# The experts' w1 and w3 laid out in pairs of rows: 4 KB DMA runs where there were 2 KB

## The chip, the cores and the metric

The kernel runs as one program on one core of a Trainium2 chip. The metric is the device time of an execution in microseconds (us), the median of three runs. One execution was taken by the hardware profiler; all rows in this document up to the prediction come from that execution. It reports the engines PE (TensorE matmuls), PEld (its weight loads), DVE (VectorE), ACT (ScalarE), POOL (GpSimd), SP (SyncE, which here only issues DMAs) and the core's 16 DMA engines.

## The reference

One step of a hybrid decoder for 2048 prompt tokens and 8 x 4 sample tokens, D = 1024, all float32: stick-breaking attention beside an RG-LRU, an output projection, and then the part that matters here, a mixture of 32 experts of which each token uses two:

```python
def expert_block(args):
    toks, e = args
    xb = x_pad[toks]
    hb = jax.nn.silu(xb @ w1[e]) * (xb @ w3[e])   # w1, w3: 1024 x 512
    return hb @ w2[e]                             # w2: 512 x 1024
...
out = out.reshape(n_rows, d) * row_gate[:, None].astype(x.dtype)
return jax.ops.segment_sum(out, row_tok, num_segments=n_tok + 1)[:n_tok]
```

Every expert's w1, w3 and w2 are 2 MB each (2048 KB), 6.29 million bytes (MB) in all, and are read from HBM once. A final residual add and RMSNorm end the step.

## The kernel before

The phases follow one another: modulation, input projection, attention, then `router_experts_phase`, then `final_phase`. The router writes each token's row twice into scratch tensors in HBM, `xs_d0` and `xs_d1` (half a row each), sorted by expert. `experts_of` then goes through the 32 experts in order and, for each, through as many blocks of 64 rows as that expert has (a loop with a register as its bound; it is one block for some experts and four for others).

A block n needs these steps, each on an engine of its own:

- POOL, `load(n)`: four DMAs of 64 KB bring the block's rows from `xs_d` into `x_in` (it lies in `rowsP`, two buffers), line L1935. Each of the four parts has a semaphore of its own, and `hold` makes POOL wait, before it issues a part, until the same part of the block before has landed. So only one DMA of each part is under way at a time.
- POOL, `store(n)`: two DMAs of 128 KB write a finished block to `ys_d`, L1949. Before it issues them POOL waits until both DMAs of the store before have landed. Loads and stores alternate in POOL's order.
- ACT, `landed(n + 1)`: when all four parts have landed, one copy of the rows into `o_rs` (L1987); DVE turns it into `xT` (in `o_sq`, L2051).
- PE, `hidden`: x times w1 and w3, L2016. The work is cut into strips: 64 calls for a block, which stand as 128 records. ACT and DVE form silu and the product (L1992, L2056 to L2060).
- PE, `out`: the hidden rows times w2, L2023, 64 records. ACT copies the result into `y` (L1997).

The weights come on SP's queue into three slots: `w13_0` to `w13_2` hold w1 and w3 together, `w2_0` to `w2_2` hold w2. In the trace's names `w13_0` and the `w2` slots stand as `w`, `w13_1` lies in `oT` and `w13_2` in `w_out`. SP issues, for expert e, the two DMAs of w1 and w3 (2048 KB each, L1913) once `hidden` of expert e - 3 has freed the slot, and then four DMAs of 512 KB for w2 (L1922) once expert e - 3 is finished. PE waits for an expert's w1 and w3 before its first block and for its w2 before `out`. Expert 0's weights are loaded ahead, during the router. After expert 31's weights SP loads `x1_d` rows for the final phase (L1926 to L1931) into slots that come free.

In w13 partition p holds eight rows of w1 and w3, rows 8p to 8p + 7, of 2 KB each; row c of w1 lies beside row c of w3. w2's rows are 4 KB.

Of the kernel before, what the change touches and what calls it, by code (L numbers as in the profile page):

```python
# [15 lines left out]
P = 128  # L16
D = 1024
KC = D // P
# [15 lines left out]
DE = D // 2  # L34
# [3 lines left out]
Q = P // STRIPS  # L38
# [272 lines left out]
def emptied(n, engine):  # L311

    return sum(e == engine for _, e in JOBS[:n + 1])
# [532 lines left out]
def attention_phase(nc, io, keep, sems):  # L846
# [15 lines left out]
    def place(n):  # L862

        return divmod(n - FIRST, WINDOW) if n >= FIRST else (-1, 0)

    EVENTS = []
    for n in range(TICKS):
        unit, p = place(n)
# [15 lines left out]

    with ExitStack() as stack:
        k = Kit(nc, stack)
        shared = keep["w13_0"][:, :, :, :].rearrange("p c a n -> p (c a n)")
        kT = [shared[:, SEQ * i:SEQ * i + SEQ] for i in range(2)]
        qT = [shared[:, SEQ * (2 + i):SEQ * (2 + i) + SEQ] for i in range(2)]
        vv = [k.sb(f"vv{i}", [P, NT, P]) for i in range(2)]  # L890
# [34 lines left out]
        ident, oT = keep["ident"], keep["oT"]  # L925
# [497 lines left out]
def router(nc, io, keep, sems, k):  # L1423
# [6 lines left out]
    w_out = keep["w_out"]  # L1430
# [8 lines left out]
    t1, xT = mid[:, 2 * D:3 * D], mid[:, 3 * D:].rearrange("p (c n) -> p c n", c=KC)  # L1439
# [32 lines left out]
    ident, oT = keep["ident"], keep["oT"]  # L1472
# [10 lines left out]
    def sync(sp):  # L1483
        sp.dma_start(nf_row[:, :], io["norm_ffn"].to_broadcast([P, D])).then_inc(s["small"], 16)

        def load_x(i):
            if i == 0:
                sp.dma_start(x_t[0][0:NS, :], io["x_sample"].rearrange("b t n -> (b t) n")).then_inc(s_x[0], 16)
            else:
                sp.dma_start(x_t[i % 2][:, :], x_src[i - 1]).then_inc(s_x[i % 2], 16)  # L1490

        def load_rg(i):
            sp.dma_start(featT[i % 2][:, FC:, :], rgT[i - 1]).then_inc(s_rg[i % 2], 16)

        load_rg(1)
        load_x(0)
        sp.dma_start(w_r[:, :, 0:NG], io["w_group"][0].rearrange("(c p) n -> p c n", p=P)).then_inc(s["wr"], 16)
        sp.dma_start(w_r[:, :, 8:RW], io["w_router"][0].rearrange("(c p) n -> p c n", p=P)).then_inc(s["wr"], 16)
        sp.dma_start(b_r[:, 0:NG], io["b_group"].to_broadcast([P, NG])).then_inc(s["small"], 16)
        sp.dma_start(b_r[:, 8:RW], io["b_router"].to_broadcast([P, NE])).then_inc(s["small"], 16)  # L1500
        load_x(1)
        load_rg(2)
        for at, name in enumerate(("w1", "w3")):
            sp.dma_start(keep["w13_0"][:, :, at, :], io[name][0, 0].rearrange("(p c) n -> p c n", p=P)).then_inc(sems["pre"], 16)
        for i in range(NTL):
            sp.wait_ge(s["x1"], i + 1)
            sp.dma_start(io["x1_d"][row0[i]:row0[i] + size[i], :], x1[i % 2][0:size[i], :]).then_inc(s_st[i % 2], 16)
            if i + 2 < NTL:
                load_x(i + 2)
            if i >= 1 and i + 2 < NTL:  # L1510
                sp.wait_ge(s["mm1"], i + 1)
                load_rg(i + 2)
        for b in range(2):
            sp.wait_ge(s_st[b], 16 * len(range(b, NTL, 2)))
# [337 lines left out]
def experts_of(nc, io, keep, sems, k, emptied, gates_scalar, gates_vector):  # L1852
# [7 lines left out]
    w13, w2 = [keep[f"w13_{i}"] for i in range(SLOTS)], [keep[f"w2_{i}"] for i in range(SLOTS)]  # L1860
    x_in = keep["rowsP"][:, 2, :].rearrange("p (a n) -> p a n", a=2)
    x_turn = keep["o_rs"][:, :, :].rearrange("p c n -> p (c n)")
    xT = keep["o_sq"][:, :, :].rearrange("p c n -> p (c n)").rearrange("p (c u b) -> p c u b", c=KC, u=UNITS)
# [3 lines left out]
    yb, h = keep["banks"][3], [keep["banks"][b] for b in (4, 6)]  # L1867
# [4 lines left out]
    s_w13 = [k.sem(f"p7_w13{i}") for i in range(SLOTS)]  # L1872
    s_w2 = [k.sem(f"p7_w2{i}") for i in range(SLOTS)]
    src = {n: io[n][0] for n in ("w1", "w3", "w2")}
# [17 lines left out]
    def sync(sp):  # L1892
        done = sp.alloc_register("blocks_done")
        sp.reg_mov(done, 0)
        emptied(sp, "low")
        for j in range(EC):
            sp.dma_start(w2[0][:, j, :], src["w2"][0].rearrange("(p j) n -> j p n", p=P)[j]).then_inc(s_w2[0], 16)
        sp.wait_ge(sems["placed"], 1)
        for landed in s_in:
            sp.wait_ge(landed, 32)  # L1900
        for e in range(NE):
            i = e % SLOTS
            if e == 1:
                emptied(sp, "oT")
            if e == 2:
                emptied(sp, "w_out")
            if e >= SLOTS:
                sp.reg_add(done, done, blocks_of(sp, e - SLOTS))
                freed = sp.snap(done, min_val=1, max_val=MAX_BLOCKS)
                hold(sp, s["h1"], freed, s["sp"])  # L1910
            if e > 0:
                for at, name in enumerate(("w1", "w3")):
                    sp.dma_start(w13[i][:, :, at, :], src[name][e].rearrange("(p c) n -> p c n", p=P)).then_inc(s_w13[i], 16)  # L1913
            if e == 1:
                emptied(sp, "mid")
            if e == 2:
                emptied(sp, "high")
            if e >= SLOTS:
                hold(sp, s["y"], freed, s["sp"])
            if e > 0:  # L1920
                for j in range(EC):
                    sp.dma_start(w2[i][:, j, :], src["w2"][e].rearrange("(p j) n -> j p n", p=P)[j]).then_inc(s_w2[i], 16)  # L1922
        x1_rows = io["x1_d"][0:SEQ, :].rearrange("(t p) n -> p t n", p=P)
        sp.reg_add(done, done, blocks_of(sp, NE - 3))
        hold(sp, s["y"], sp.snap(done, min_val=1, max_val=MAX_BLOCKS), s["sp"])
        sp.dma_start(keep["x1_a"], x1_rows[:, 0:8, :]).then_inc(sems["x1_a"], 16)  # L1926
        sp.dma_start(keep["x1_b"], x1_rows[:, 8:12, :]).then_inc(sems["x1_b"], 16)
        sp.reg_add(done, done, blocks_of(sp, NE - 2))
        hold(sp, s["y"], sp.snap(done, min_val=1, max_val=MAX_BLOCKS), s["sp"])
        sp.dma_start(keep["x1_c"], x1_rows[:, 12:16, :]).then_inc(sems["x1_c"], 16)  # L1930
        sp.dma_start(keep["x1_s"], io["x1_d"][SEQ:, :]).then_inc(sems["x1_s"], 16)  # L1931
# [79 lines left out]
    def tensor(pe):  # L2011
        def hidden(i, u):

            for c in range(KC):
                for q in range(STRIPS):
                    mm = pe.matmul(h[u][q * Q:q * Q + Q, 0:2 * P], xT[:, c, u, :], w13[i][:, c, :, q * P:q * P + P], start=(c == 0), stop=(c == KC - 1))  # L2016
            return mm

        def out(i, u):

            for j in range(EC):
                for q in range(STRIPS):
                    mm = pe.matmul(yb[q * Q:q * Q + Q, u * (XW // 2):(u + 1) * (XW // 2)], hT[:, u, j, :], w2[i][:, j, q * (XW // 2):(q + 1) * (XW // 2)],  # L2023
                                   start=(j == 0), stop=(j == EC - 1))
            return mm

        def body(n, e, b, extra):
            i = e % SLOTS
            for u in range(UNITS):
                pe.wait_ge(s["xT"], 2 * n + u + 2)  # L2030
                hidden(i, u).then_inc(s[f"h{u}"], 1)
            pe.wait_ge(s_w2[i], 16 * EC * (e // SLOTS + 1))
            for u in range(UNITS):
                pe.wait_ge(s["hT"], 2 * n + u + 1)
                mm = out(i, u)
            mm.then_inc(s["y"], 1)

        def before(e):
            i = e % SLOTS
            if e == 0:  # L2040
                pe.wait_ge(sems["pre"], 32)
            else:
                pe.wait_ge(s_w13[i], 32 * (e // SLOTS + (1 if i else 0)))

        pe.wait_ge(sems["placed"], 1)
        experts(pe, body, before)
# [177 lines left out]
def build_program(nc, io):  # L2224
    with ExitStack() as stack:
        k = Kit(nc, stack, clears=False)
        keep = {
            "ident": k.sb("ident", [P, P]), "ones": k.sb("ones", [P, P]), "eps": k.sb("eps", [P, 1]),
            "vecT": k.sb("vecT", [P, NVEC]), "biasP": k.sb("biasP", [P, H]), "nbiasP": k.sb("nbiasP", [P, H]),
        }  # L2230
# [4 lines left out]
        sems = {f"w_{part}": k.sem(f"w_{part}") for part in WCOL}  # L2235
# [25 lines left out]
        keep["rowsP"] = k.sb("rowsP", [P, 4, D])  # L2261
        rows_s = k.sb("rowsS", [P, 4, D])
        keep["rowsS"], keep["rows_mem"] = rows_s[0:NS, :, :], (keep["rowsP"], rows_s)
        keep["w13_0"] = k.sb("w13_0", [P, KC, 2, DE])
        keep["oT"], keep["w_out"] = k.sb("oT", [P, FC, SEQ]), k.sb("w_out", [P, 2, KC, 512])
        for name in ("w_out0", "w_out1", "rows", "x1_a", "x1_b", "x1_c", "x1_s"):
            sems[name] = k.sem(name)
        attention_phase(nc, io, keep, sems)
        for i in range(3):
            keep[f"w2_{i}"] = k.sb(f"w2_{i}", [P, EC, D])  # L2270
        keep["w13_1"] = keep["oT"][:, :, :].rearrange("p f n -> p (f n)").rearrange("p (c a n) -> p c a n", c=KC, a=2)
        keep["w13_2"] = keep["w_out"][:, :, :, :].rearrange("p h c n -> p (h c n)").rearrange("p (c a n) -> p c a n", c=KC, a=2)
        tiles = lambda t: t[:, :, :, :].rearrange("p c a n -> p c (a n)")
        keep["x1_a"], keep["x1_b"] = tiles(keep["w13_2"]), keep["w2_2"][:, :, :]
        keep["x1_c"], keep["x1_s"] = tiles(keep["w13_0"])[:, 0:4, :], tiles(keep["w13_0"])[0:NS, 4, :]
        keep["yy"] = tiles(keep["w13_1"])
# [35 lines left out]
```

## Time and profile before

| what | value |
|---|---|
| median of 3 runs | 2826.22 us (2825.38 to 2827.81) |
| the profiled execution, its own time | 2821.11 us |
| its span, first to last instruction | 2819.6 us |
| its mean granted PE clock | 0.969 |
| PE busy | 2586.6 us (92%) |
| first `hidden` of the experts to the end of the last `out` | 1842.40 to 2724.58 us |
| moved over the whole span | 577.06 MB, mean 205 GB/s |

The experts' stretch is some 31% of the span. PE busy is near its whole length in most of it, and the DMA engines are near full as well, so that an average over the span does not say which of the two sets the pace: that has to be read in pieces. A DMA share over 1.00 means that packets of different queues overlap on an engine.

### The profile page before, as it was taken

Reading aid. Unit: us, or ns where it says so; the run is one execution under the profiler, and the core shown is the slowest. Engines: PE = TensorE matmul, PEld = TensorE weight load, DVE = VectorE, ACT = ScalarE, POOL = GpSimd, SP = SyncE. Lnnn points to the kernel's source line nnn. Section 1 sums busy time; section 2 is a strip of 40 time slices with the busy share of each in tenths; the row PEclk is TensorE's granted clock in tenths of the full one; section 3 lists DMA queues with packets and bytes.
Section 4 is the critical chain, followed back from the end, with each engine's and each line's share of the span. In section 5 each row is a group of like instructions: output and inputs, shape, how many; then the busy total and the mean of one; then the engine's idle time right before and its main releaser. Section 6 shows DMA issues by size and latency. Waiting matters only on the chain. (4 is left out here: it accounts for less than half of the span.)

```text
span 2819.6 us, 64656 instructions
## 1 busy us (share of the span) xinstructions
PE 2586.6 (92%) x23589; PEld 1361.0 (48%) x23589; DVE 1379.9 (49%) x2816; ACT 1055.4 (37%) x1938; POOL 648.4 (23%) x918
## 2 busy tenths in 40 slices
PE   6999999996799899899998999789999998899978
PEld 3444444442455445454543555445555554555533
DVE  2151423333678788687886777522222222222228
ACT  2221314121677777687773222122222221122214
POOL 0202020101021211111111222343333333333333
PEclk9999999998899999999999999899999999999989
DMA  9011111126586766767675344399999789999947
GB/s 335 15 61 44 45 45 43 62 85 244 174 271 218 264 234 224 262 213 244 225 262 187 116 140 139 143 261 295 281 301 299 210 257 306 323 309 297 305 134 315
DMA packets 297027, 577.06 MB, mean 205 GB/s; under 512 B 80278, under 2 KB 96727, under 8 KB 292812
## 3 DMA queue, kind: packets, MB, share of 16 engines
q1 hardware_dynamic: 194472, 427.99, 47.4%
q0 software_dynamic: 102016, 146.26, 16.9%
q8 instruction: 116, 1.90, 0.3%
q14 instruction: 99, 0.81, 0.1%
q10 hardware_dynamic: 324, 0.10, 0.0%
HBM read 461.12 MB, written 112.29 MB: 203 GB/s over the span
## 5 line engine op out<-in xcount | busy, mean ns | idle before, releaser
L1253 DVE TENSOR_TENSOR_SCAN left<-leave,left 128x512 f32<-128x512 f32 (+3 forms) x320 | 358.4, 1120 | 134.9 <-ACT leave L1135 134.1
L442 PE MATMUL bank<-xnT,w_in 128*128 128x512 f32 x768 | 330.3, 592 | 0.0
L2056 DVE TENSOR_TENSOR sg<-sg,bank 128x128 f32<-128x128 f32 x160 | 46.0, 288 | 562.5 <-ACT sg L1992 561.3
L2023 PE MATMUL bank<-w,hT 128*32 128x256 f32 x5120 | 297.5, 380 | 1.5 <-issue 1.1
L1056 POOL DMA_DIRECT2D w_out<-in_cache_v x256 | 137.6, 538 | 660.9 <-issue 658.6
L1935 POOL DMA_DIRECT2D rowsP<-xs_d x328 | 218.0, 665 | 200.0 <-DMA rowsP<-xs_d 111.4
L2016 PE MATMUL bank<-w,o_sq 128*32 128x256 f32 x3840 | 218.0, 384 | 30.2 <-DVE o_sq L2051 23.2
L442 PEld LDWEIGHTS bank<-xnT,w_in 128*128 128x128 f32 x768 | 145.6, 190 | 181.8 <-issue 178.9
L1992 ACT ACTIVATE sg<-bank 128x128 f32<-128x128 f32 x160 | 44.4, 278 | 501.2 <-PE bank L2016 501.2
L1619 PE MATMUL bank<-w_out,w 128*128 128x512 f32 x512 | 227.7, 597 | 1.8 <-DVE w L1683 1.8
L442 PE MATMUL bank<-w_in,xnT 128*128 128x512 f32 x512 | 220.4, 592 | 0.0
L2023 PEld LDWEIGHTS bank<-w,hT 128*32 128x32 f32 x5120 | 160.1, 110 | 124.2 <-DVE hT L2060 25.7
L2016 PE MATMUL bank<-oT,o_sq 128*32 128x256 f32 x3712 | 205.8, 379 | 7.1 <-DVE o_sq L2051 7.1
L1304 PE MATMUL tb<-ident,take 128*128 128x128 f32 x1088 | 181.7, 284 | 29.5 <-DVE take L1159 25.7
L1135 ACT ACTIVATE leave<-zb,nbiasP 128x512 f32<-128x512 f32 (+3 forms) x320 | 204.6, 639 | 8.0 <-PE zb L1297 8.0
L1137 ACT ACTIVATE take<-zb,biasP 128x512 f32<-128x512 f32 (+3 forms) x320 | 207.3, 648 | 0.0
L1159 DVE TENSOR_TENSOR take<-take,left 128x512 f32<-128x512 f32 (+3 forms) x320 | 194.6, 608 | 15.5 <-DVE left L1253 0.4
L1949 POOL DMA_DIRECT2D ys_d<-y x164 | 115.6, 709 | 365.3 <-DMA ys_d<-y 180.8
L1291 PE MATMUL zb<-w 64*128 64x512 f32 (+3 forms) x640 | 164.1, 590 | 31.0 <-ACT take L1137 19.9
L1304 PEld LDWEIGHTS tb<-ident,take 128*128 128x128 f32 x1088 | 119.8, 142 | 146.7 <-issue 77.4
L1339 PE MATMUL tb<-ident,w_out 128*128 128x128 f32 x1024 | 159.9, 280 | 25.3 <-DMA w_out<-in_cache_k 15.7
L2016 PEld LDWEIGHTS bank<-w,o_sq 128*32 128x32 f32 x3840 | 125.2, 111 | 118.2 <-DVE o_sq L2051 26.3
(408 smaller groups left out, 3402.1 us busy)
## 6 DMA issues: line engine op xcount, KB each, us to landing
w_out<-in_cache_v POOLq DMA_DIRECT2D x256, 256.0 KB
w_out<-in_cache_k SPq DMA_DIRECT2D x256, 256.0 KB
w<-in_w SPq DMA_DIRECT2D x128, 512.0 KB, 17.4
w<-in_w SPq DMA_DIRECT2D x22, 2048.0 KB, 23.1
oT<-in_w SPq DMA_DIRECT2D x22, 2048.0 KB, 24.2
w_out<-in_w SPq DMA_DIRECT2D x20, 2048.0 KB, 25.7
ys_d<-zeros SPq DMA_DIRECT2D x32, 816.0 KB
ys_d<-y POOLq DMA_DIRECT2D x166, 128.0 KB, 7.8
```

Of the source, the lines that this page charges most:

```text
L442: mm = pe.matmul(ps[:, :], w, m, start=(i == 0), stop=(i == len(parts) - 1))
L1135: act.activation(leave[n % 4][:, 0:cols], zb[n % 3][:, 0:cols], ACT.Sigmoid, scale=-SCALE, bias=keep["nbiasP"][:, head:head + 1]).then_inc ...
L1137: act.activation(take[n % 4][:, 0:cols], zb[n % 3][:, 0:cols], ACT.Sigmoid, scale=SCALE, bias=keep["biasP"][:, head:head + 1]).then_inc(s_ ...
L1159: dve.tensor_tensor(take[n % 4][:, 0:cols], take[n % 4][:, 0:cols], left[n % 4][:, 1:cols + 1], ALU.mult).then_inc(s_w, 1)
L1253: dve.tensor_tensor_scan(left[n % 4][:, 0:cols][:, ::-1], leave[n % 4][:, 0:cols][:, ::-1], leave[n % 4][:, 0:cols][:, ::-1], left[n % 4][ ...
L1291: mm = pe.matmul(zb[(n + par) % 3][:, 0:cols], qT[pair % 2][half, t * P:t * P + P], kT[pair % 2][half, c * GRP:c * GRP + cols], start=True ...
L1304: mm = pe.transpose(to[:, j * P:j * P + P], take[n % 4][:, j * P:j * P + P], ident[:, :])
L1339: mm = pe.transpose(to[:, i * P:i * P + P], kp[g % 2][:, i, f * P:f * P + P], ident[:, :])
L1619: mm = pe.matmul(pb[half][0:n, :], lhs, w_out[:, half, c, :], start=(c == 0), stop=(c == KC - 1))
L1935: return pool.dma_start(x_in[64 * half:64 * half + 64, buffer, u * (XW // 2):(u + 1) * (XW // 2)].rearrange("p a n -> p (a n)"), in_strips ...
L2016: mm = pe.matmul(h[u][q * Q:q * Q + Q, 0:2 * P], xT[:, c, u, :], w13[i][:, c, :, q * P:q * P + P], start=(c == 0), stop=(c == KC - 1))
L2023: mm = pe.matmul(yb[q * Q:q * Q + Q, u * (XW // 2):(u + 1) * (XW // 2)], hT[:, u, j, :], w2[i][:, j, q * (XW // 2):(q + 1) * (XW // 2)], s ...
```

## The change

A partition's eight rows of w1, and of w3, are kept as four pairs; the two rows of a pair lie side by side in SBUF, then the pair of w3. A pair is 4 KB in one piece on both sides of the DMA. `hidden` takes row c from pair c // 2, place c % 2. The same number of DMAs with the same bytes is issued at the same places, and PE gets the same matmuls on the same numbers. No instruction moves on any engine. The other users of the memory (`x1_a`, `x1_c`, `yy`, the attention's `kT` and `qT`) keep their flat layout.

```diff
@@ router, the first expert's weights
         for at, name in enumerate(("w1", "w3")):
-            sp.dma_start(keep["w13_0"][:, :, at, :], io[name][0, 0].rearrange("(p c) n -> p c n", p=P)).then_inc(sems["pre"], 16)
+            sp.dma_start(keep["w13_0"][:, :, at, :, :].rearrange("p c two n -> p c (two n)"),
+                         io[name][0, 0].rearrange("(p c two) n -> p c (two n)", p=P, two=2)).then_inc(sems["pre"], 16)
@@ experts_of, sync
                 for at, name in enumerate(("w1", "w3")):
-                    sp.dma_start(w13[i][:, :, at, :], src[name][e].rearrange("(p c) n -> p c n", p=P)).then_inc(s_w13[i], 16)
+                    sp.dma_start(w13[i][:, :, at, :, :].rearrange("p c two n -> p c (two n)"),
+                                 src[name][e].rearrange("(p c two) n -> p c (two n)", p=P, two=2)).then_inc(s_w13[i], 16)
@@ experts_of, tensor
-                    mm = pe.matmul(h[u][q * Q:q * Q + Q, 0:2 * P], xT[:, c, u, :], w13[i][:, c, :, q * P:q * P + P], start=(c == 0), stop=(c == KC - 1))
+                    mm = pe.matmul(h[u][q * Q:q * Q + Q, 0:2 * P], xT[:, c, u, :], w13[i][:, c // 2, :, c % 2, q * P:q * P + P], start=(c == 0), stop=(c == KC - 1))
@@ build_program
-        keep["w13_0"] = k.sb("w13_0", [P, KC, 2, DE])
+        keep["w13_0"] = k.sb("w13_0", [P, KC // 2, 2, 2, DE])
```

## Rows read from the trace of the kernel before

**Rows 1.** Page: the costliest groups of instructions, two of them.

```profile
L2056 DVE TENSOR_TENSOR sg<-sg,bank 128x128 f32<-128x128 f32 x160 | 46.0, 288 | 562.5 <-ACT sg L1992 561.3
L1992 ACT ACTIVATE sg<-bank 128x128 f32<-128x128 f32 x160 | 44.4, 278 | 501.2 <-PE bank L2016 501.2
```

**Rows 2.** Stretches of the experts' part: busy us by engine, clock, DMA share, GB/s.

```profile
core 0: us, PE busy (x) PEld busy (x) DVE busy (x) ACT busy (x) POOL busy (x), PEclk, DMA share, GB/s
2000.00:2200.00 200.00, 196.69 (x3600) 115.19 (x3596) 51.55 (x149) 43.47 (x75) 75.19 (x111) 1.00 1.06 297
2200.00:2350.00 150.00, 150.00 (x2768) 88.45 (x2764) 39.81 (x115) 32.82 (x57) 59.69 (x88) 1.00 0.82 239
2350.00:2450.00 100.00, 80.56 (x1396) 46.83 (x1392) 21.09 (x61) 17.69 (x30) 29.81 (x45) 0.90 1.06 320
```

**Rows 3.** PE in order of time: start, us, what, idle before; around the longest waits.

```profile
2363.95 7.09 PE L2016 MATMUL bank<-oT,o_sq 128*32 128x256 f32 x128
2370.85 3.69 PE L2023 MATMUL bank<-w,hT 128*32 128x256 f32 x64
2387.93 8.80 PE L2016 MATMUL bank<-w_out,o_sq 128*32 128x256 f32 x128 [13.38 <-DMA w_out<-in_w]
...
2406.31 9.84 PE L2016 MATMUL bank<-w,o_sq 128*32 128x256 f32 x128 [6.06 <-DMA w<-in_w]
2415.97 3.69 PE L2023 MATMUL bank<-w,hT 128*32 128x256 f32 x64
2419.48 7.09 PE L2016 MATMUL bank<-w,o_sq 128*32 128x256 f32 x128
```

**Rows 4.** Waits, 1842 to 2725 us: who for whom, us, times, longest.

```profile
ACT o_rs L1987 <- DMA rowsP<-xs_d: 59.5, 53, 4.0
...
PE bank L2016 <- DVE o_sq L2051: 32.3, 13, 20.2
...
PE bank L2016 <- DMA w_out<-in_w: 15.4, 2, 13.4
PE bank L2016 <- DMA w<-in_w: 6.1, 1, 6.1
```

**Rows 5.** DMA, 2050 to 2200 us: the weights' queue q1 (packets, MB, share).

```profile
q1 hardware_dynamic: 15742, 37.05, 85.7%
```

**Rows 6.** DMA, 2416 to 2420 us: w1 and w3 arriving nearly alone.

```profile
q1 hardware_dynamic: 741, 1.49, 102.6%
```

**Rows 7.** DMA, 213 to 215 us, another phase: 4 KB packets alone.

```profile
q1 hardware_dynamic: 204, 0.84, 101.7%
```

**Rows 8.** DMA, 2160 to 2163 us: loads of x beside 2 KB packets, us to landing.

```profile
q1 hardware_dynamic: 464, 0.93, 94.6%
rowsP<-xs_d POOLq DMA_DIRECT2D x4, 64.0 KB, 8.6
```

**Rows 9.** DMA, 2118 to 2121 us: loads of x issued as w2 arrives.

```profile
rowsP<-xs_d POOLq DMA_DIRECT2D x3, 64.0 KB, 11.4
```

**Rows 10.** DMA, 2670 to 2690 us: x1 rows, all of 4 KB, arriving.

```profile
q1 hardware_dynamic: 1207, 4.75, 80.9%
rowsP<-xs_d POOLq DMA_DIRECT2D x7, 64.0 KB, 11.8
```

**Rows 11.** DMA, 2700 to 2709 us: no weights under way.

```profile
rowsP<-xs_d POOLq DMA_DIRECT2D x5, 64.0 KB, 3.9
```

**Rows 12.** POOL in order of time, beside the x1 rows.

```profile
2665.89 0.65 POOL L1935 DMA_DIRECT2D rowsP<-xs_d  x1 [1.03 <-DMA rowsP<-xs_d]
...
2678.70 0.65 POOL L1935 DMA_DIRECT2D rowsP<-xs_d  x1 [1.02 <-DMA rowsP<-xs_d]
```

**Rows 13.** PE in order of time, beside the x1 rows and after them.

```profile
2667.18 7.11 PE L2016 MATMUL bank<-w,o_sq 128*32 128x256 f32 x128
...
2679.95 7.11 PE L2016 MATMUL bank<-oT,o_sq 128*32 128x256 f32 x128 [2.14 <-DVE o_sq L2051]
2693.09 7.11 PE L2016 MATMUL bank<-oT,o_sq 128*32 128x256 f32 x128 [2.52 <-DVE o_sq L2051]
2703.54 7.09 PE L2016 MATMUL bank<-oT,o_sq 128*32 128x256 f32 x128
2713.96 7.09 PE L2016 MATMUL bank<-oT,o_sq 128*32 128x256 f32 x128
2720.87 3.71 PE L2023 MATMUL bank<-w,hT 128*32 128x256 f32 x64
```

More of the change, by code:

```diff
@@ L886, in attention_phase @@
         k = Kit(nc, stack)
-        shared = keep["w13_0"][:, :, :, :].rearrange("p c a n -> p (c a n)")
+        shared = keep["w13_0"][:, :, :, :, :].rearrange("p c a two n -> p (c a two n)")
         kT = [shared[:, SEQ * i:SEQ * i + SEQ] for i in range(2)]
@@ L2270, in build_program @@
             keep[f"w2_{i}"] = k.sb(f"w2_{i}", [P, EC, D])
-        keep["w13_1"] = keep["oT"][:, :, :].rearrange("p f n -> p (f n)").rearrange("p (c a n) -> p c a n", c=KC, a=2)
-        keep["w13_2"] = keep["w_out"][:, :, :, :].rearrange("p h c n -> p (h c n)").rearrange("p (c a n) -> p c a n", c=KC, a=2)
-        tiles = lambda t: t[:, :, :, :].rearrange("p c a n -> p c (a n)")
+        keep["w13_1"] = keep["oT"][:, :, :].rearrange("p f n -> p (f n)").rearrange("p (c a two n) -> p c a two n", c=KC // 2, a=2, two=2)
+        keep["w13_2"] = keep["w_out"][:, :, :, :].rearrange("p h c n -> p (h c n)").rearrange("p (c a two n) -> p c a two n", c=KC // 2, a=2, two=2)
+        tiles = lambda t: t[:, :, :, :, :].rearrange("p c a two n -> p (c a) (two n)")
         keep["x1_a"], keep["x1_b"] = tiles(keep["w13_2"]), keep["w2_2"][:, :, :]
```

## The prediction

> **What bounds the kernel now.** I began with the stretches [rows 2]. From 2000 to 2200 us PE is busy for 196.69 of 200 us with the DMA engines full (share 1.06). From 2200 to 2350 PE has no gap at all and DMA has room (0.82): the weights are ahead. From 2350 to 2450 it is the other way round: PE busy 80.56 of 100 us, its clock at 0.90, DMA full. So two limits of nearly one size alternate.
>
> Then PE in order of time. Undisturbed blocks follow each other every 10.4 us: 2703.54 to 2713.96 is 10.42 [rows 13]. ACT's gate stands 160 times, two for each block [rows 1], so there are 80 blocks, and 80 x 10.43 = 834 us. The part takes 1842.40 to 2724.58, 882 us, so 48 us are lost. Where: three blocks from 2363.95 start at 2387.93, 2406.31 and 2419.48 [rows 3]: 23.98 + 18.38 + 13.17, less 3 x 10.43, is 24.2 us over, by waits of 13.38 and 6.06 us for w1 and w3, and by matmuls at the half clock of 1.2 GHz after the wait (8.80 and 9.84 us for a group of 7.09). One more wait of some 2 us for `w_out` is in the waits (15.4 us in 2) [rows 4]; about **27 us** are thus lost to late weights. PE's waits for `xT` (`o_sq`) are 32.3 us in 13, of which 20.2 is the wait ahead of the first block [rows 4]: 12 us in 12 waits are the second loss. The rest, 9 us, is a slow first block and small gaps.
>
> The waits of ACT's copy decide the argument: it waits for the DMA of x in 53 of some 80 blocks, though only 59.5 us in total [rows 4]. The next block's rows arrive just before they are needed. **The load of x has almost no slack**, and it shares the DMA engines with the weights.
>
> **What the change removes.** An expert's w1 and w3 are 2048 packets of 2 KB; they become 1024 of 4 KB. Alone, 741 packets of 2 KB took 4 us on 16 engines: 64000 / 741 = 86.4 ns each [rows 6], and 204 of 4 KB took 2 us: 156.9 ns [rows 7]. I take 160 for the latter, since the window's edges cut packets. Two small ones cost 172.8, so 12.8 ns are saved per pair, 7.4%: 1024 x 12.8 / 16 = 0.82 us for an expert, 25 us of DMA time over the 31 that arrive in this part.
>
> In mixed traffic q1 moves 37.05 MB in 150 us, 247 GB/s [rows 5]; an expert's 6.29 MB takes 25.5 us. Two thirds of it get 7.4% cheaper, so 4.9% in all; and if blocks slow by some 6%, the x and y queue leaves about 1% more. That is 263 GB/s and 23.9 us. Seven experts or so arrive between the last slack and the long waits, so of 27 us lost, 7 x 1.6 = 11 to 13 are won back and **14 stay** (bounds: nothing won; all 27 won). In the 150 us from 2200 the DMA has room, so there nothing is gained.
>
> The Trainium skill, "DMA: Bandwidth & Descriptors", Specifications, gives 512 B as the smallest transfer for line rate. By that alone the term would be zero; the measured 172.8 against 160 ns decides for the 25 us.
>
> PE's moving operand has the same two runs of 128 numbers, only farther apart; the DMAs' number, places and issue instructions stay. Nothing else changes cost: I put these at 0. Expert 0's weights arrive during the router, far ahead of the first `hidden`, which waits for `o_sq` and not for them [rows 4].
>
> **What the change adds.** A load of x lands 3.9 us after its issue when no weights are under way [rows 11], 8.6 us after it beside 2 KB packets [rows 8], 11.4 when it is issued as w2's 4 KB packets arrive and its later part still runs beside 2 KB ones [rows 9], and 11.8 us beside nothing but 4 KB packets [rows 10]. The size of the neighbour's packets matters, as if each small packet of the x and y queue waited for one packet of the weights, whatever its size.
>
> That is a rule of the Trainium skill too ("DMA: Bandwidth & Descriptors", Queues, rings and completion order): an engine goes round its queues packet by packet. By that rule the 4.7 us that small neighbours add (8.6 less 3.9) are the turns of 54 packets, and 54 turns of 160 ns would add 8.7 us; the rows' 7.9 (11.8 less 3.9) about agrees.
>
> What it does to a block: POOL holds a part until the same part of the block before has landed. Part 4 is issued at 2665.89 and again at 2678.70, 12.81 us later [rows 12], and PE's blocks follow at 12.77 and 13.14 us (2667.18, 2679.95, 2693.09) [rows 13], with waits of 2.14 and 2.52 for `xT`. At 8.6 us to landing the same round is 8.6 + 0.65 (issue) = 9.3, below PE's 10.43; at a landing of 9.8 the two are equal. Today a third of the bytes come in 4 KB packets and mostly the slow landings are made good by the next fast one. After the change there is no fast one while weights are under way.
>
> The cycle beside weights: 11.4 + 0.65 = 12.1 us. I take 11.4 rather than 11.8 because x1's rows, read at a large pitch, may load the queue in another way; 12.8 is the upper bound, 10.43 (no effect) the lower. With no weights under way a round is 3.9 + 0.65 = 4.6, and the two buffers of x let such fast rounds make good some slow ones. So I average. An expert has 80 / 32 = 2.5 blocks; with a mean block cycle C, weights are under way for 23.9 / (2.5 C) = 9.56 / C of the time. C = 4.6 + (12.1 - 4.6) x 9.56 / C gives C = 2.3 + sqrt(5.3 + 71.7) = 11.07 us. That is above 10.43, so x sets the pace on average.
>
> **Sum.** 80 x 11.07 = 886; weights still late, 14; slow first block, 3: 903 us against 882, **+21 us**. The profiled execution took 2821.1 us and would take 2842; the median shown is 5.1 us above it, so 2847. Nothing changes after the part: the final phase starts with POOL's gathers when the experts are done, and moves with it.
>
> **Rivals.**
>
> 1. *x's load stays in its slack (faster).* Its round is paid only once per block, and idle weight queues (0.82 from 2200 on) give it time back; if C stays at 10.43 the loads cost nothing, and 11 to 27 us of late weights are won, perhaps 5 of PE's waits too: around -17, 2809. For it: w2's packets are large already and PE's waits for x come to only 12 us. Against it: 53 waits of ACT. It decides below C = (882 - 17) / 80 = 10.81.
> 2. *No change.* C lands near 10.8, gain and loss cancel: 2826.
> 3. *Full slowdown.* The x1 stretch is typical: 12.9 us a block whenever weights are under way, and 4 KB packets go no faster in it than 4.75 MB in 20 us, 237 GB/s, 26.5 us an expert [rows 10]. Then weights hardly ever pause; with C = 12.9 they take 26.5 of 32.2 us, and by the same average C = 2.3 + sqrt(5.3 + 8.3 x 10.6) = 11.96: 957 + 3, +78, 2904.
> 4. *The 4 KB runs are not made* (the descriptors stay at 2 KB). Then nothing changes. w2's rows of 4 KB stand as 4 KB packets in the mean packet size (37.05 MB in 15742 packets is 2.4 KB, what 2048 small and 512 large ones give) [rows 5], so I give this 0.02, within rival 2.
>
> **How the numbers follow.** Forecast (C 10.95 to 11.4, +10 to +45) 0.45; rival 1 0.25; rival 2 0.13; rival 3 0.17. The forecast's own range is 2836 to 2871. The range for 8 in 10 leaves out the far ends of rivals 1 and 3: 2805 to 2888. A measurement of this kernel tells a difference from about 0.2%, 5.7 us. Faster by more has rival 1 (0.25), slower the forecast and rival 3 (0.62), within it 0.13.
>
> **What would show it.** In the changed kernel: q1's packets in the experts' part fall from 15742 in 150 us to some 9000 to 9700, with a mean of 4 KB (right: rival 4 falls). Loads of x land at a median of 10 to 11.5 us over the part, where the rows show 8.6 beside small packets. PE waits for `o_sq` grow from 12 us to some 50 or more, in 30 to 50 waits of 1 to 2.5 us, in stretches with DMA share over 1; the DMA share falls below 1 more often. The waits for `w_out` and `w` from in_w fall from 21.5 to about 10. If x's median landing stays under 9.8 us, the forecast is wrong and rival 1 holds. If 4 KB packets take well under 160 ns in mixed traffic or the queue of x is served before them, the landing won't rise.

## The result: 1.6% slower

The changed kernel takes 2874.35 us, the median of 3 runs (2868.15 to 2874.9), against 2826.22; the ratio is 1.0163 with a 95% interval of 1.0140 to 1.0186. The profiled execution has a span of 2866.7 us, 47.1 above the one before. Of these, 42.8 lie in the experts' part: it runs from 1845.63 to 2770.65 us, 925.0, where it was 882.2 ([rows 13] and the section on time before). 3.2 us lie ahead of it and 1.0 behind.

PE's busy time in the changed kernel, in the first two stretches of [rows 2] and with its columns:

```profile
2000.00:2200.00 200.00, 184.10 (x3356) 106.36 (x3348) 48.12 (x139) 38.13 (x69) 71.31 (x105) 1.00 0.92 275
2200.00:2350.00 150.00, 143.01 (x2616) 82.73 (x2612) 37.77 (x109) 31.62 (x55) 55.14 (x82) 1.00 0.75 222
```

From 2000 to 2200 us PE is busy for 184 us where it was 197, and the DMA engines have become *less* busy, 0.92 where they were 1.06. So neither the DMA engines nor PE alone set the pace over this stretch. (The share of one queue alone can stand at 103%, as the row at 2455 us below shows, so that a share a little over 1.00 is not by itself a sign of two queues.) Who waits for whom in the changed kernel, 1842 to 2775 us, as in [rows 4]:

```profile
POOL ys_d L1951 <- DMA ys_d<-y: 198.6, 52, 7.3
ACT o_rs L1989 <- DMA rowsP<-xs_d: 167.7, 67, 27.1
...
PE bank L2018 <- DVE o_sq L2053: 83.0, 46, 20.3
...
PE bank L2018 <- DMA w<-in_w: 11.0, 1, 11.0
```

The first of PE's waits for `o_sq` is 20.3 us as before; the other 45 take 62.7 us where 12 took 12. Late weights cost 11.0 us of waiting where they cost 21.5. Both changes that were forecast are there, and the loss is the larger.

The queue of the weights, 2050 to 2200 us, as in [rows 5], and then two microseconds (2455 to 2457) in which they arrive alone, as in [rows 6]:

```profile
q1 hardware_dynamic: 9055, 34.88, 72.9%
```

```profile
q1 hardware_dynamic: 202, 0.82, 103.0%
```

34.88 MB in 9055 packets is 3.9 KB each: the 4 KB runs were made. Alone, 202 of them take 2 us, 158 ns each, where two of 2 KB took 172.8 [rows 6]. Where weights flow all the time, from 2091 to 2126 us, these are the loads of x and the weights, and POOL and PE in order of time:

```profile
q1 hardware_dynamic: 2481, 9.69, 85.5%
...
rowsP<-xs_d POOLq DMA_DIRECT2D x12, 64.0 KB, 11.4
```

```profile
2102.14 0.65 POOL L1937 DMA_DIRECT2D rowsP<-xs_d  x1 [2.06 <-DMA rowsP<-xs_d]
...
2114.36 0.65 POOL L1937 DMA_DIRECT2D rowsP<-xs_d  x1 [2.25 <-DMA rowsP<-xs_d]
```

```profile
2091.31 7.11 PE L2018 MATMUL bank<-w_out,o_sq 128*32 128x256 f32 x128 [1.61 <-DVE o_sq L2053]
...
2103.39 7.11 PE L2018 MATMUL bank<-w_out,o_sq 128*32 128x256 f32 x128 [1.45 <-DVE o_sq L2053]
...
2115.60 7.11 PE L2018 MATMUL bank<-w,o_sq 128*32 128x256 f32 x128 [1.59 <-DVE o_sq L2053]
...
2126.05 7.09 PE L2018 MATMUL bank<-w,o_sq 128*32 128x256 f32 x128
```

Loads of x land after 11.4 us, the same part is issued again after 12.22 us (2102.14, 2114.36), and PE's blocks follow at 12.08 and 12.21 us with a wait of 1.5 us each. A matmul group takes 7.1 us as before, so PE itself is not slower. At 2126.05 the wait is gone: the share of the weights' queue fell to 0.41 from 2110 to 2112 us, and the four loads issued from 2108.23 to 2114.36 landed after 6.7 to 9.1 us.

### The profile page after: what moved, and what is told of

It reads as the page before. It is cut to its first block and busy times, and to the rows that moved or that the text cites. A ratio compares the mean times of both kernels' runs of the same rounds, so it can differ in the third digit from the quotient of the medians.

```text
span 2866.7 us, 64656 instructions
## 1 busy us (share of the span) xinstructions
PE 2595.4 (91%) x23589; PEld 1358.8 (47%) x23589; DVE 1380.4 (48%) x2816; ACT 1050.7 (37%) x1938; POOL 650.1 (23%) x918
## 5 line engine op out<-in xcount | busy, mean ns | idle before, releaser
L1951 POOL DMA_DIRECT2D ys_d<-y x164 | 115.8, 710 | 353.4 <-DMA ys_d<-y 198.6
## 6 DMA issues: line engine op xcount, KB each, us to landing
w<-in_w SPq DMA_DIRECT2D x128, 512.0 KB, 20.3
w_out<-in_w SPq DMA_DIRECT2D x20, 2048.0 KB, 20.3
```

## The experiments

Theory: a load of x waits, for each packet of its queue, for one weight packet of whatever size, and its round (time to landing plus issue) is PE's pace once it is above 10.43 us. Rivals: PE or SBUF handles pairs of rows more slowly; the DMAs' number or rate matters; only the share of large packets beyond a threshold does. In the changed kernel q0, the queue of x and y, carries five packets of 16 bytes for each one of 4 KB; "small packets" in the expectations are these.

The diffs show the main lines only. What follows from them is left out: the counts that PE and DVE wait for, and, in the first three runs, the same edit for expert 0 in the router.

**Undo the packets, keep the layout.**

```diff
-                    sp.dma_start(w13[i][:, :, at, :, :].rearrange("p c two n -> p c (two n)"),
-                                 src[name][e].rearrange("(p c two) n -> p c (two n)", p=P, two=2)).then_inc(s_w13[i], 16)
+                    for two in range(2):
+                        sp.dma_start(w13[i][:, :, at, two, :],
+                                     src[name][e].rearrange("(p c two) n -> p c two n", p=P, two=2)[:, :, two, :]).then_inc(s_w13[i], 16)
```

> The pair layout in SBUF stays and PE reads it as in the changed kernel, but w1 and w3 arrive in packets of 2 KB: each in two DMAs of 1024 KB, one for the even and one for the odd rows (four DMAs an expert where there were two). Theory (a load of x waits for one weight packet per small packet of its own, so the packet size is what costs): back to the kernel before, 2822 to 2832 us, loads of x landing at 8.6 us beside 2 KB packets, PE's waits for o_sq near 32 us in all. Rival (PE reads pairs of rows, or SBUF takes them, more slowly): stays at 2860 to 2880. Rival (the number of DMAs matters): differs from both.

2824.86 us, ratio to before 0.9998 (0.9984 to 1.0012). The waits:

```profile
PE bank L2020 <- DVE o_sq L2055: 31.4, 13, 20.1
...
PE bank L2020 <- DMA w_out<-in_w: 12.5, 2, 11.9
...
PE bank L2020 <- DMA w<-in_w: 6.3, 1, 6.3
```

13 waits for `o_sq`, 31.4 us: the kernel before to a microsecond, with PE reading pairs. The layout costs nothing that can be told; with the control below, the packets are all of it.

**The control: as many DMAs, but 4 KB.**

```diff
-                    sp.dma_start(w13[i][:, :, at, :, :].rearrange("p c two n -> p c (two n)"),
-                                 src[name][e].rearrange("(p c two) n -> p c (two n)", p=P, two=2)).then_inc(s_w13[i], 16)
+                    for part in range(2):
+                        sp.dma_start(w13[i][:, 2 * part:2 * part + 2, at, :, :].rearrange("p c two n -> p c (two n)"),
+                                     src[name][e].rearrange("(p c two) n -> p c (two n)", p=P, two=2)[:, 2 * part:2 * part + 2, :]).then_inc(s_w13[i], 16)
```

> Control for the run with 2 KB packets: the changed kernel with w1 and w3 in four DMAs of 1024 KB too, but each of 4 KB runs. Theory: as the changed kernel, 2865 to 2880 us. Rival (the number of DMAs is what counts): near the 2 KB run with four DMAs.

2870.72 us, ratio 1.0166 (1.0141 to 1.0191), as the changed kernel. The number of DMAs doesn't matter.

**Packets of 8 KB.**

```diff
-        keep["w13_0"] = k.sb("w13_0", [P, KC // 2, 2, 2, DE])
+        keep["w13_0"] = k.sb("w13_0", [P, KC // 4, 2, 4, DE])
...
-                                 src[name][e].rearrange("(p c two) n -> p c (two n)", p=P, two=2)).then_inc(s_w13[i], 16)
+                                 src[name][e].rearrange("(p c two) n -> p c (two n)", p=P, two=4)).then_inc(s_w13[i], 16)
```

> w1 and w3 lie in fours of rows, so that their runs are 8 KB. Theory: if packets of 8 KB are made, a load of x beside them lands after some 17 to 20 us (3.9 plus 8 times 8/4), a block beside w1 and w3 takes about that long, and the kernel is 150 to 280 us slower than before, 2975 to 3105 us. Rival (larger packets cost only the one time, or the queues are served by bytes and not by packets): at most 2880.

2927.39 us, ratio 1.0343 (1.0305 to 1.0382): the right way and past the rival's 2880, but 103 us over the kernel before measured beside it (2824.08) instead of 150 to 280. The weights' queue from 2050 to 2200 us, and loads of x from 1850 to 2700 us (least, median, most us to landing), and PE:

```profile
q1 hardware_dynamic: 6176, 33.61, 67.0%
```

```profile
DMA to landing us min/median/max: 3.4/9.4/18.0
```

```profile
2116.54 7.11 PE L2018 MATMUL bank<-w_out,o_sq 128*32 128x256 f32 x128 [1.21 <-DVE o_sq L2053]
...
2133.59 9.25 PE L2018 MATMUL bank<-w_out,o_sq 128*32 128x256 f32 x128 [6.43 <-DVE o_sq L2053]
...
2146.17 7.09 PE L2018 MATMUL bank<-w,o_sq 128*32 128x256 f32 x128
```

The mean packet is 5.4 KB, w2's of 4 KB included, and the trace has 15864 packets of 8192 bytes, so they were made. The slowest landing is 18.0 us, but landings of 17 to 20 us were worked out as the rule beside w1 and w3: only 11 of 324 loads take 16 us or more, and 139 take under 5. While PE waits, the weights fill their three slots and stop, and the next loads land early: the weights' queue has no packet under way in 281 of the 986.5 us of the experts' part (169 of 925.0 in the changed kernel, 75 of 882.2 before). The loss limits itself. That is what my figure for this run lacked. After the wait of 6.43 us the next group takes 9.25 us instead of 7.1, at a mean granted clock of 0.76 from 2133.59 to 2142.84, so that part of it ran at 1.2 GHz.

**All weights in 2 KB**, the kernel before with w2 cut as well.

```diff
                 for j in range(EC):
-                    sp.dma_start(w2[i][:, j, :], src["w2"][e].rearrange("(p j) n -> j p n", p=P)[j]).then_inc(s_w2[i], 16)
+                    rows, cols = slice(j // 2 * 2, j // 2 * 2 + 2), slice(j % 2 * 512, j % 2 * 512 + 512)
+                    sp.dma_start(w2[i][:, rows, cols], src["w2"][e].rearrange("(p j) n -> p j n", p=P)[:, rows, cols]).then_inc(s_w2[i], 16)
```

> The kernel before with w2 in 2 KB packets as well (four DMAs of 512 KB as before, each for two of the four rows of a partition and half of the columns), so that no weight packet in the experts' part is of 4 KB. Theory: no load of x lands after more than about 9.5 us, PE's waits for o_sq lose most of their 12 us beyond the first; against that w2 takes 7% longer, up to 0.4 us an expert, and the waits for late weights grow by some 3 to 8 us: 2815 to 2830 us. Rival (2 KB packets cost DMA rate and nothing is won): 2830 to 2845.

2822.28 us, ratio 0.9990 (0.9976 to 1.0004): no difference that can be told. PE's waits:

```profile
PE bank L2017 <- DVE o_sq L2052: 25.1, 4, 20.3
...
PE bank L2017 <- DMA w_out<-in_w: 17.2, 2, 13.7
...
PE bank L2017 <- DMA w<-in_w: 4.2, 1, 4.2
```

The waits for `o_sq` fell from 32.3 to 25.1 us, as expected. The waits for late weights did not grow by 3 to 8 us: they are 21.4 us, as against 21.5 before [rows 4]. Loads of x issued up to 2640 us land after at most 10.6 us, not 9.5; beside x1's rows, which stay at 4 KB, after up to 12.8.

**Two thirds of the bytes large, in two ways.** First w1 large, w3 small (`at == 0` as in the change, `at == 1` as in the first experiment), then w1 and w3 as in the change with w2 cut as just shown.

> The changed kernel with w1 in 4 KB packets and w3 in 2 KB ones (two DMAs of 1024 KB for w3); w2 stays at 4 KB. So two thirds of the weight bytes come in large packets, where it was one third before and all after. Theory (each large packet costs a turn of the loads of x): about half of the loss, 2838 to 2858 us. Rival (a threshold: the loss appears once all are large, since any fast landing makes a slow one good): within 0.3% of the kernel before.

> The changed kernel with w2 in 2 KB packets. Again two thirds of the weight bytes in large packets, but in one stretch of some 15 us for an expert, longer than a load of x is under way. Theory: between before and after, 2845 to 2868 us, and not better than the run in which w1 is large and w3 small, since a whole round of x falls beside large packets. Rival (w2's packets were never the matter): as the changed kernel, 2868 to 2876.

2843.22 us, ratio 1.0060 (1.0040 to 1.0080), and 2849.29 us, 1.0073 (1.0046 to 1.0100). Loss and share go together: nothing that can be told with none or one third large, 0.6% and 0.7% with two thirds, 1.6% with all. No threshold shows, and w2's packets count: with w1 and w3 large, cutting w2 alone wins back about half. The two ways can't be told apart within their intervals.

**Without the stores of the results.** Both kernels without the DMAs to `ys_d`, with a semaphore of the same values in their place; the final phase reads what lay in `ys_d`, so the output rows are not the experts' sums.

```diff
-            for u in range(UNITS):
-                pool.dma_start(in_strips(io["ys_d"], n * G + G, u),
-                               y[:, ds(n & 1, 1), u * (XW // 2):(u + 1) * (XW // 2)].rearrange("p a n -> p (a n)")).then_inc(s["st"], 16)
+            pool.nop().then_inc(s["st"], 32)
```

> The changed kernel (4 KB packets) without the stores of the experts' results to ys_d: the final phase reads what lay there. Half of the small queue's packets are gone. Theory (the loads of x wait for turns behind small packets of their own queue, each of which waits for one weight packet): x lands at a median of 7 to 9.5 us, so the round is below 10.43 us, PE's waits for o_sq fall from 83 to under 35 us, and the time is 2780 to 2805 us. Rival (the 4 KB packets slow something else on PE's path, or landing depends on the rate of the weights alone): above 2840.

> The kernel before (2 KB packets) without the stores of the experts' results. Theory: x had little to win (12 us), late weights get some of the freed DMA time: 2785 to 2812 us, equal to or slower than the 4 KB kernel without stores by up to 12 us, because with slack in x's loads only the better rate of large packets is left. Rival (large packets are worse in themselves): clearly faster than the 4 KB kernel without stores.

4 KB: 2801.0 us, ratio to before 0.9906 (0.9882 to 0.9931). 2 KB: 2798.53 us, 0.9900 (0.9874 to 0.9927). PE's waits with 4 KB packets and no stores:

```profile
PE bank L2018 <- DVE o_sq L2053: 21.4, 4, 19.9
...
PE bank L2018 <- DMA w_out<-in_w: 8.4, 1, 8.4
...
PE bank L2018 <- DMA w<-in_w: 4.8, 1, 4.8
```

and its loads of x, 1850 to 2700 us:

```profile
DMA to landing us min/median/max: 3.5/9.0/13.0
```

With the stores' packets gone, loads of x beside 4 KB packets land at a median of 9.0 us (10.8 with stores), and 28% of them take more than the 9.8 us at which they decide (57% with stores). **The difference of 1.6% between 4 KB and 2 KB is gone**: the two kernels are 2.5 us apart, within their intervals. The large packets' better rate shows at best in the late weights (13.2 us of waiting; 15.9 in the 2 KB kernel without stores) and not in the time. Taking the stores away also takes away POOL's waits for them, so that this pair does not say how much of the difference was turns in the queue and how much was POOL standing at `hold` for a store. That second path is real: in the changed kernel POOL waits 198.6 us for stores to land, 180.8 before.

**Smaller everywhere, and smaller still.** First w2, as above, and x1's rows in 2 KB too (`x1_a` is shown; `x1_b` and `x1_c` are cut in the same way), then w1 and w3 in 1 KB (the kernel before with each of their DMAs cut into two halves of the columns).

```diff
-        sp.dma_start(keep["x1_a"], x1_rows[:, 0:8, :]).then_inc(sems["x1_a"], 16)
+        for cols in (slice(0, 512), slice(512, 1024)):
+            sp.dma_start(keep["x1_a"][:, :, cols], x1_rows[:, 0:8, cols]).then_inc(sems["x1_a"], 16)
...
```

> The kernel before with w2 in 2 KB packets (as in the earlier run) and the loads of x1's rows in 2 KB packets as well (two DMAs of half the columns for each). Theory: the x waits of 2.14 and 2.52 us beside x1's rows go too, late weights stay at some 24 us; 0.1% to 0.4% faster than before, 2816 to 2824 us. Rival (smaller packets lose as much rate as they give slack): within 0.1%.

> The kernel before with w1 and w3 in 1 KB packets (each in two DMAs, of half the columns). Theory of turns: loads of x beside them land earlier than 8.6 us, PE's waits for o_sq fall; but a packet of 1 KB costs more than half of one of 2 KB, the weights come some 5% later and PE's waits for late weights rise from 21.5 us to 30 or more: 2826 to 2850 us. Rival (large packets alone are bad, the smaller the better): faster than before by over 0.3%.

All 2 KB: 2819.0 us, ratio 0.9968 (0.9956 to 0.9980), **faster than both kernels**. 1 KB: 2830.71 us, ratio 1.0016 (1.0002 to 1.0030). The interval of the first overlaps that of the run in which x1's rows stay at 4 KB (0.9976 to 1.0004), so that the share of x1's rows in the gain isn't shown. In the first the waits for `o_sq` are down to the first one and one more:

```profile
PE bank L2020 <- DVE o_sq L2055: 21.4, 2, 20.4
...
PE bank L2020 <- DMA w_out<-in_w: 16.6, 2, 14.4
...
PE bank L2020 <- DMA w<-in_w: 4.5, 1, 4.5
```

so that late weights cost 21.1 us, no more than before. In the second they take more, while loads of x land earlier (a median of 8.6 us from 1850 to 2700 us, 9.4 before):

```profile
PE bank L2017 <- DVE o_sq L2052: 26.0, 5, 20.4
...
PE bank L2017 <- DMA w_out<-in_w: 14.6, 2, 8.2
...
PE bank L2017 <- DMA w<-in_w: 8.0, 1, 8.0
...
PE bank L2017 <- DMA oT<-in_w: 6.0, 2, 4.0
```

These are 28.6 us of waiting for late weights, as against 21.5 before [rows 4] (30 or more were expected): the other side of the trade.

## Why the prediction had the way right and the size wrong

The forecast was +21 us, 2847; measured were +48 us, 2874.35.

**Right.** Which wait would grow and which would shrink; the packets' cost alone (160 ns taken, 158 measured); the cycle beside weights, 12.1 taken, 12.08 and 12.21 in the rows. Undoing the packets gave all of the time back. Landing beside 4 KB packets came out at 11.4 us as taken; that was a choice between the rows' 11.4 and 11.8, and no run tests its reason (x1's pitch). The late weights came out at the 14 us that were said to stay:

```profile
2419.08 7.11 PE L2018 MATMUL bank<-w_out,o_sq 128*32 128x256 f32 x128 [2.02 <-DVE o_sq L2053]
...
2441.04 9.58 PE L2018 MATMUL bank<-w,o_sq 128*32 128x256 f32 x128 [11.02 <-DMA w<-in_w]
...
2453.96 7.09 PE L2018 MATMUL bank<-w,o_sq 128*32 128x256 f32 x128
```

One block is over by 11.53 and the next, at the low clock, by 2.5, 14.0 in all. That the cheaper packets brought this is not shown: PE was also slower, which gives the weights time, and without the stores, where PE has one pace in both, 4 KB packets have only 2.7 us less of these waits. The prediction's figure was also rounded its own way: 7 x 1.6 is 11, and 24.2 + 2 is 26, so that 14 to 16 us were to stay.

**Wrong: the average over fast and slow rounds.** The failed step is "C = 4.6 + (12.1 - 4.6) x 9.56 / C gives C = 2.3 + sqrt(5.3 + 71.7) = 11.07 us". It let each round of 4.6 us with no weights under way pay back slow ones in full. In the trace PE's blocks follow at 10.42 us or more, whatever x does, and x has two buffers only. After a pause of the weights one to three blocks start on time and then the 12.1 us are back: 48 of 79 steps from block to block are longer than 10.6 us, with a median of 12.07, and the others are at PE's own 10.43. The measured term: 925.0 less 14.0 for late weights and 5.9 for the first block is 905.1, 11.31 for each of 80 blocks instead of 11.07 (inside the 10.95 to 11.4 that the forecast was given, at its slow end). That is 19 us of the 22 by which the experts' part was over the forecast (43 against 21); the first block, 5.9 instead of 3, is the other 3.

With no repayment at all, C = 10.43 + (12.1 - 10.43) x 9.56 / C gives 11.79, and the measured 11.31 lies two thirds of the way from there to 11.07. With the weights' measured 277 GB/s (22.7 us an expert) the two ends are 11.72 and 10.87, and it lies half way. So fast rounds do repay, but only in part. How far each gap repays was read from the trace and not isolated by a run.

That an average hides this shows in the landings themselves. Over the experts' part the mean time to landing is 9.1 us before, 9.0 with 4 KB packets and 8.9 with 8 KB, while the kernel gets slower by 48 and 103 us; the share of loads that take over 9.8 us goes from 36% to 57% and 46%, with slower ones among them. For the same reason the sign that the prediction set, a median landing under or over 9.8 us, is a weak one: with 8 KB packets the median was 9.4, as in the kernel before.

**Outside the part**, put at 0: 3.2 us ahead and 1.0 behind in the profiled execution. The runs with w1 and w3 untouched in the router start their experts' part at 1847 to 1857 us in their profiles, later still, so the 3.2 us are nothing that the change must explain.

**The rivals.** Faster (x within its slack) fell: it holds only when the stores are gone, and even then large packets win nothing that shows. Full slowdown fell too: the weights' rate from 2091 to 2126 us is 9.69 MB in 35 us, 277 GB/s, above my 263 and far above x1's 237, so they finish early and pause often (no weight packet under way in 169 of 925.0 us). x1's cycle of 12.8 to 13.1 us [rows 13] was not typical.

**The mechanism, as far as it is shown.** That the size of the weights' packets sets the landing of x is shown by the runs. That it does so by one weight packet for each packet of x's queue can be held against the traces. From 1850 to 2700 us q0 sent 67030 packets in the kernel before while 310 loads of x, four to a block, were issued: 54 packets for a block on each of the 16 engines, the number that the prediction had from the landings. Without the stores it is 36 (45794 packets, 316 loads). The loads are sorted by what the weights' queue did while they were under way (over three quarters busy, over 95% of its bytes in one size):

| weight packets beside the load | loads | median landing, us | 3.9 us and one weight packet each |
|---|---|---|---|
| none (changed kernel) | 45 | 4.2 | 3.9 |
| 1 KB | 108 | 8.0 | 54 x 0.046 + 3.9 = 6.4 |
| 2 KB (kernel before) | 83 | 8.7 | 54 x 0.0864 + 3.9 = 8.6 |
| 4 KB (changed kernel) | 196 | 11.4 | 54 x 0.158 + 3.9 = 12.4 |
| 2 KB, no stores | 75 | 8.6 | 36 x 0.0864 + 3.9 = 7.0 |
| 4 KB, no stores | 222 | 9.6 | 36 x 0.158 + 3.9 = 9.6 |

The last column is an estimate (0.046 us is the time of a 1 KB packet in the one microsecond where they came alone). The order is right; in three rows it is off by 1.0 to 1.6 us, so one packet for one packet is not all of it.

The rule of the Trainium skill ("DMA: Bandwidth & Descriptors", Queues, rings and completion order), that an engine takes queues in turn packet by packet, agrees with this order from 1 KB to 4 KB and with the slower kernel at 8 KB. No run shows single turns, since the packets' rows don't name their engine.

## What to carry to other kernels

Before making a transfer's packets larger, ask who shares its DMA engines. Here a stream with one transfer of each part in flight at a time got slower with its neighbour's packet size, though the neighbour itself, while it flowed, got faster. Compare time to landing beside small and beside large packets, add the issue, and hold that against the consumer's own pace. And don't average a limit that has a floor: a fast round pays back only what the buffers can hold.

## What was not expected of the hardware

- The weights move faster beside the small queue in 4 KB packets (277 GB/s from 2091 to 2126 us, 247 before [rows 5]), more than the 7% saved alone; a part may be that blocks, and with them loads and stores, come slower.
- 8 KB packets beside small ones cost only 3.4%; the weights then pause longer (share of their queue 67.0% from 2050 to 2200 us, 85.7% before).
- 1 KB packets cost 0.16% of the time: 36.25 MB in 26926 packets from 2050 to 2200 us, 242 GB/s, against 247 with 2 KB ones [rows 5]:

```profile
q1 hardware_dynamic: 26926, 36.25, 88.1%
```
